# A decoder trunk's first unit: the narrow tile's first column group goes between the norms of steps 2 and 3

## The reference

```
h = rmsnorm(x, pre_norm[0])                    # x: 8 sample rows, 16 meta rows, 1024 prompt rows
proj = h @ w_in                                # 1024 x (512 + 512 + 1024 + 1024 + 16)
q, k, v, r, g_low = split(proj)
log_alpha = log_sigmoid(g_low @ w_gate_up + b_gate) / 16
...                                            # chunked scan over q, k, v, log_alpha
x = x + rmsnorm(mixer_output @ w_out, post_norm[0])
```

## Time and profile before

| what | value |
|---|---|
| median of 3 runs | 1514.11 us (1513.77 to 1514.53) |
| the profiled execution's own time | 1509.73 us |
| its span, first to last instruction | 1508.0 us |
| mean granted TensorE clock over the span | 0.983 of full speed |
| PE busy | 1416.8 us, 94% of the span |
| DVE, ACT, POOL busy | 1166.0, 837.3, 241.6 us |

### The profile page before, as it was taken

How to read it: one execution, slowest core, us unless ns; L and a number is a source line. 1 busy time by engine, 2 the same in 40 slices (tenths; PEclk the granted TensorE clock), 3 DMA queues, 4 the chain that set the end, 5 groups by cost and what they waited for, 6 DMA issues and landing times. The chain is left out here.

```text
span 1508.0 us, 31302 instructions
## 1 busy us (share of the span) xinstructions
PE 1416.8 (94%) x11554; PEld 1179.1 (78%) x11554; DVE 1166.0 (77%) x2591; ACT 837.3 (56%) x1877; POOL 241.6 (16%) x424
## 2 busy tenths in 40 slices
PE   5989999799999969999999999989999999999987
PEld 5889887667888759898888988867777777777765
DVE  4556587758877887968977898995889787588786
ACT  4745555356556545546655665664655556465453
POOL 5010122001332100012111112121011211000002
PEclk8999999999999999999999999999999999999999
DMA  6465557355585433448844764753485574555453
GB/s 191 126 217 145 173 171 220 96 164 165 150 202 182 128 117 108 140 107 214 251 128 125 237 200 145 212 160 98 144 264 163 152 212 131 161 155 174 139 190 63
DMA packets 283874, 245.77 MB, mean 163 GB/s; under 512 B 32664, under 2 KB 250876, under 8 KB 283052
## 3 DMA queue, kind: packets, MB, share of 16 engines
q1 hardware_dynamic: 273628, 209.36, 47.1%
q0 software_dynamic: 10096, 34.41, 8.7%
HBM read 183.02 MB, written 65.00 MB: 164 GB/s over the span
## 5 line engine op out<-in xcount | busy, mean ns | idle before, releaser
L1482 PE MATMUL bank<-h,w 128*128 128x268 f32 (+1 forms) x4752 | 834.9, 330 | 22.8 <-ACT w L867 16.0
L1482 PEld LDWEIGHTS bank<-h,w 128*128 128x128 f32 x4752 | 701.5, 192 | 100.4 <-issue 25.5
L883 DVE TENSOR_TENSOR w<-w_raw,w 128x1024 fp32r<-128x1024 f32 x132 | 160.9, 1219 | 37.7 <-ACT w L867 37.2
L852 PE MATMUL bank<-s_w_out,s_yt_hi 128*128 128x512 f32 (+2 forms) x544 | 168.1, 398 | 2.0 <-DVE s_ys L2600 1.7
L867 ACT ACTIVATE w<-w_raw 128x1024 fp32r<-128x1024 f32 x132 | 138.7, 1051 | 7.3 <-DMA w_raw<-in_ssd_w_in_dram 7.3
L1560 DVE SCALAR_TENSOR_TENSOR conv<-before_conv,cw,conv 128x260 f32<-128x260 f32 (+2 forms) x216 | 125.3, 580 | 4.3
L852 PEld LDWEIGHTS bank<-s_w_out,s_yt_hi 128*128 128x128 f32 (+2 forms) x544 | 95.9, 180 | 28.4 <-issue 2.5
L852 PE MATMUL bank<-g_w_out,g_ot_hi 128*128 128x512 f32 (+2 forms) x288 | 97.2, 426 | 1.1 <-DVE g_ot_lo L2118 0.9
L852 PE MATMUL bank<-s_w_out,s_yt_lo 128*128 128x512 f32 x240 | 94.7, 395 | 0.0
L2363 ACT ACTIVATE s_decay<-s_decay,t_ac 128x128 f32<-128x128 f32 (+1 forms) x288 | 85.5, 379 | 1.2
L1528 ACT ACTIVATE conv<-bank,cw 128x268 f32<-128x268 f32 (+1 forms) x72 | 45.8, 637 | 72.2 <-PE bank L1482 55.3
(11 more groups left out here) (259 smaller groups left out, 2458.8 us busy)
## 6 DMA issues: line engine op xcount, KB each, us to landing
w_raw<-in_ssd_w_in_dram SPq DMA_DIRECT2D x80, 512.0 KB, 4.3
w_raw<-in_gla_w_in_dram SPq DMA_DIRECT2D x48, 512.0 KB, 4.5
s_decay<-kept_acd SPq DMA_DIRECT2D x32, 512.0 KB, 6.3
w_raw<-in_ssd_w_out_dram SPq DMA_DIRECT2D x30, 512.0 KB, 4.1
g_chunk<-kept_gq SPq DMA_DIRECT2D x32, 448.0 KB, 5.2
s_chunk<-kept_sq SPq DMA_DIRECT2D x32, 384.0 KB, 4.9
kept_sq<-stage SPq DMA_DIRECT2D x80, 134.0 KB, 4.4
kept_sq<-stage SPq DMA_DIRECT2D x40, 256.0 KB, 4.8
```

Source lines behind the costliest of these rows:

```text
L852: last = pe.matmul(bank[0:r, :], yt[a][:, k, 0:r], wo[:, b, 512 * half:512 * half + 512], start=(k + a + b == 0), stop=(k == tiles - 1 and ...
L883: dve.tensor_tensor(self.part(i, 1), self.raw(i), hi, ALU.subtract).then_inc(self.w_lo, 1)
L1482: last = pe.matmul(bank[:, 0:n], w[:, p.tile % 2, a, k, :], h[:, b, k, c:c + n], start=(i == 0), stop=(i == len(terms) - 1))
```

## The change

The first unit's list now has the norms of steps 0 to 2 (pieces 0 to 5), the narrow tile's first column group (piece 6), the norms of steps 3 and 4 (pieces 7 to 10), "consts" (11), and the narrow tile's second column group (12). From piece 13 on the list is as it was. The extra wait for the two pieces ahead is now made by both pieces of the narrow tile and not only by the first. The other three units with u = 0 keep their order. Two of them have one column group and so one narrow piece, for which nothing is new. Unit (1, 0, 0), the first of layer 1 (steps 0 to 4 again), has two, pieces 118 and 119, with nothing between them: the second now waits also for piece 117, a norm, and for piece 118, the narrow tile's own first half. That one counts as freed when ACT (`Sizes.act_low`, L1252) and then DVE (`Sizes.dve_low`, L1257) have read its bank.

```diff
--- before.py
+++ after.py
@@ -148,9 +148,10 @@
 
         if u == 0:
             steps, b = GROUP_STEPS[G], len(pieces)
-            for s in steps:
-                for half in range(2):
-                    pieces.append(Piece("norm", L, G, u, s, half))
+            def norms(part):
+                pieces.extend(Piece("norm", L, G, u, s, half) for s in part for half in range(2))
+
+            norms(steps if b else steps[0:3])
             if b:
                 lead, gap = {(0, 1): (12, 2), (1, 0): (8, 1), (1, 1): (20, 4)}[(L, G)]
                 for i, s in enumerate(steps):
@@ -165,10 +166,13 @@
                         self.before(2 * i, [("n_scale", L, steps[i + 1])])
                     if i + 2 < len(steps):
                         self.before(2 * i, [("n_square", L, steps[i + 2])])
-            if (L, G) == (0, 0):
-                pieces.append(Piece("consts", L, G, u, -1, 0))
             self.low[(L, G)] = len(self.tiles)
             tile(TILES[L], "low")
+            if not b:
+                second = pieces.pop()
+                norms(steps[3:5])
+                pieces.append(Piece("consts", L, G, u, -1, 0))
+                pieces.append(second)
         if L == 0:
             if (G, u) == (0, 1):
                 for half in range(2):
@@ -1458,10 +1462,10 @@
                 a = self.channel(p, 2 * p.j + x)
                 last = pe.transpose(bank[0:11, x * P:(x + 1) * P], self.m["cvp"][:, a, :], self.m["ident"][:, :])
         else:
+            if part == 0 and p.kind == "low":
+                self.wait_free(pe, i - 2)
+                self.wait_free(pe, i - 1)
             if part == 0 and self.plan.first_of[p.tile] == i:
-                if p.kind == "low":
-                    self.wait_free(pe, i - 2)
-                    self.wait_free(pe, i - 1)
                 pe.wait_ge(self.W.w_hi, self.W.index[("in", p.tile)] + 1)
             last = self.project(pe, p, part, bank, self.plan.first_of[p.tile] == i)
             if part < PARTS - 1:
```

## The result

The changed kernel takes 1517.38 us (median of 20 runs, 1512.17 to 1521.76), the kernel before 1511.78 us (20 runs, 1509.24 to 1520.08). The ratio is 1.0031, 95% interval 1.0021 to 1.0041: 4.7 us slower, between 3.2 and 6.2. The whole interval lies above the 0.2% that I had set as the bound of "no change". The forecast was +2.7 us. It had the right sign, and the range of 1514.3 to 1519.3 us holds the time, but it called "within 0.2%" the likeliest, and this is slower by over 0.2%. That 1517.38 lies so near 1516.8 is partly luck: my base, the median of three runs, was 2.3 us above the median of 20, and that made up for most of what the sum was short of.

A forecast was written before the change was run, and what follows sets the result against it. PE, busy 94% of the span, was taken as the bound, so its idle time counts. +0.7 us (opening) and +2.0 us (piece 119) on 1514.11 us gave 1516.8 us, range 1514.3 to 1519.3 us.

The forecast's parts named there:

- the sum: Whole kernel: +0.7 and +2.0 make +2.7 us, added to 1514.11 us for a forecast of 1516.8 us.
- The early projection isn't early: Opening: the projection needs piece 5 drained, so PE starts at 20.38 us as before and the wait grows.
- Term 1: Opening: 3.86 us before the first projection becomes a 4.6 us chain after its 24 matmuls, +0.7 us.
- about 2.8 us of work: Opening chain: PE's work within its 4.6 us, taken as enough for the clock to stay up.
- I pass it on whole: After the opening: later work takes its data from these pieces, so the whole +0.7 us reaches the total.
- Term 2: Unit (1, 0, 0): piece 119 waits for piece 118 to be read, PE idle from 571.3 to 573.28, +2.0 us.
- Rival 1: Opening: clock falls between the first and second narrow pieces, 2.5 us more, +5.2, 1519.3 us; chance 0.12.
- Rival 2: Opening: clock returns in the middle of the first narrow piece, gaining 1.3 us; +1.4, 1515.5 us; chance 0.08.
- Rival 3: Behind 571 us: later waits absorb term 2, or ACT reads the bank sooner; +0.7, 1514.8 us; chance 0.12.
- Rival 4: Same mechanism, terms larger by some tenths (ACT and DVE chain 0.4 us longer); +3.1 to +3.6, about 1517.5 us; chance 0.24.
- Rival 5: Opening ends 2 us sooner, term 2 absorbed, a later clock loss goes away; 1510.5 us, faster; chance 0.02.
- 4 us at half level: Around 88 us: a stretch at the lower clock, used by rival 5 to price a clock loss at 1.7 us.

## Why the prediction was right or wrong

- **The early projection isn't early, and the drain of piece 5 is why.** Right. 4.26 us of idle time of PE stands ahead of the 24 matmuls, and moving that drain alone brought their start from 20.45 to 18.35.
- **Term 1, the chain of 4.6 us.** The path was right up to its last wait, which DVE's drain ended and not ACT's copies; the size was not: 4.0 us. I took the small weights' transposes at the 1.0 us of the earlier trace rows, and they took 0.65 at the upper level; the fourth half started 1.85 us behind the projection, not 2.04. With a later start of the matmuls (20.62) and a piece of 5.30 instead of 5.5 us, the opening costs 0.1 to 0.2 us at its end, not 0.7. The chain's "about 2.8 us of work" doesn't follow from the rows that I named, which give 1.25 + 1.25 + 1.0 = 3.5; the chain measured 1.47 + 0.66 + 0.65 = 2.8.
- **"The work after it takes its data from these pieces, so I pass it on whole."** This is the step that failed. By 84 us, where PE waits for a transfer in any case, the opening costs nothing (71.9 us on the mean of four profiles with the changed opening against 71.7 of four with the old, each spread over about 1 us). Yet the time is 2.1 us longer in two sets of runs. What my sum left out is that a changed opening changes when the clock rises, and so when it falls farther on. That share is shown for one place, 1.1 us near 87 us, in four of five profiles. The other 1 us is not shown. It may be the same thing at later places: from 45 to 1490 us the lower level lasts 34 to 44 us in the five profiles of the old order (38 on the mean) and 41 to 51 in the five of the changed one (45), but the two groups overlap, and the sets' intervals are 3 to 4 us wide. It stays open.
- **Term 2, +2.0 us at piece 119, passed on whole.** Right: 1.67 to 1.85 us of idle time ended by DVE's read in five profiles, +2.7 and +1.5 us in the two sets that have it alone, and the idle time of 1.35 us behind it unchanged.
- **The sum.** The parts measured alone, 2.1 for the opening and 2.1 for the wait, make 4.2 us, and both together measured 4.7 and 5.0: within the intervals, they add up. My +2.7 was 2 us short, 1.4 of it in the opening (0.7 against 2.1).
- **Rival 1** (the clock falls between the narrow pieces) didn't happen: the second narrow piece is the first 24 of 72 matmuls that took 9.09 us together. The transposes of the chain kept the clock: the granted clock stayed at 1.00, and the small weights' eight took 0.65 us (1.0 at the lower level in the earlier trace rows). The rule of the Trainium skill (TensorE: Matmul & The Clock Gate, Part 4: PE-mode transpose), that transposes don't engage the clock gate, is not what this trace shows. **Rival 2** happened in part: the 24 matmuls took 5.30, 4.98, 4.47 and 5.13 us in four profiles of this opening, so the clock came back 0.6 to 1.7 us ahead of their end, which is a gain of 0.2 to 1.0 us on my 5.5 and not 1.3. **Rival 3** (term 2 absorbed) is out. **Rival 4** named about the right number, 1517.5, and the wrong reason; it stood on a longer chain, and the chain was shorter. **Rival 5** didn't happen, and for the reason that I had set against it, the drain of piece 5; with that drain first and step 3's transposes kept ahead, an early projection does pay. (The "4 us at half level" that it names are 3.4 in the earlier trace rows.)

## What to carry to other kernels

To fill a wait with other work, look first at what that work waits for: here it waited for the same drain, one place down in the same queue, and the cure was to move the drain (and keep the transposes that already filled part of the wait), which, with the added wait left out, turned +4.7 into -4 us. A condition that is loosened for one unit has to be read for all units that share the code: half of the loss came from a piece 550 us away. And a sum of local terms was 2 us short in 1500 here. A rise of the clock that comes 1 or 2 us sooner or later moves its falls relative to PE's idle times, and one such fall was worth 1.1 us; that part needs many runs, and a comparison of the same stretch in several profiles. The same comparison guards against a false cause: ten extra matmuls seemed to move the fall, and the place measure and the rise showed that they hadn't.

## What the runs showed of the hardware

Unchanged work took two different times. At the transposes near 84 us PE is idle for 2.4 us. Where the clock fell 0.4 to 1.4 us ahead of the end of that idle time (five profiles), it stayed at the lower level for 6.8 us; where it fell at most 0.3 us ahead of the end, or behind it (nine profiles), for 3.4 us. The first cost 1.1 us more in 169. Both came with either order of the pieces. Eighteen matmuls of extra work moved the fall to behind the idle time, in one profile. The wait for a transfer at 84 us hid added work of PE: with 1.25 us more the transposes behind it came no later, within the 1.4 us by which that place varies, and with 2.25 us more they came 1.5 us later, and about 0.4 us of the wait was left in both. Transposes alone kept the clock up: in the changed kernel's chain the granted clock stayed at 1.00. And one profiled execution of a kernel can't stand for it at this scale: the profiled executions lay 9.4 us of span apart where the kernels' medians differ by 5.6.
